# A two-layer diffusion step with 16 experts per layer: TensorE's loop over pairs of experts written out

## Chip, cores and metric

One core of a Trainium2 chip runs the whole step. The metric is the device time of one execution in microseconds; of several executions, their median.

## What is computed

Two layers (`DEPTH = 2`) of a hybrid network on 640 tokens of width 1024: 512 latent tokens and 128 context tokens, all in float32. Each layer has a mixing half (attention, a long convolution, a gated MLP; the change does not touch it) and an expert half. The expert half, cut from the reference:

```python
def _expert_choice(h, router_w, w1, w3, w2):
    ...
    C = max(1, EC_CAPACITY * N // N_EXPERTS)
    aff = jax.nn.softmax((xs @ router_w).astype(jnp.float32), axis=-1)
    gate, idx = lax.top_k(aff.T, C)
    xe = xs[idx]
    he = jax.nn.silu(jnp.einsum('ecd,edf->ecf', xe, w1)) * jnp.einsum('ecd,edf->ecf', xe, w3)
    ye = jnp.einsum('ecf,efd->ecd', he, w2) * gate[..., None].astype(h.dtype)
    out = jnp.zeros_like(xs).at[idx.reshape(-1)].add(ye.reshape(-1, D))
```

There are 16 experts. Each picks its best 64 latent and 16 context tokens (`CAP` = 80 rows), gathers them, and multiplies them with three 1024 x 1024 matrices of its own: w1, w3, w2. So every layer reads 48 matrices of 4 MiB, 201 MB.

## The kernel before

The kernel is written per engine, with semaphores for all order between engines. In the expert half the five instruction streams are these.

**TensorE** (line 1212, `expert`). Line 1177, `products`, is one product of 80 rows with a 1024 x 1024 matrix: 8 chunks of the contraction, each with 12 matmul calls (3 groups of 32 rows by 4 quarters of the columns) at line 1189. In the records each call is two MATMULs and two LDWEIGHTS, so a chunk is 24 MATMULs, a product 192, an expert 576. Four quarters of the array, 32 columns each, work side by side. An expert is: product w3 of this expert, with the 8 transposes of the next expert's gathered rows (line 1208) after its second chunk; product w1 of the next expert; product w2 of this one. Before each half of a product TensorE waits for that half of the weights (line 1182); before w1 it waits for the next rows, scaled (line 1216), and for the silu that empties the banks (line 1217); before w2 for the hidden rows (line 1219). Experts 0 to 13 are seven passes of a hardware loop of two experts each (lines 1225 to 1227); experts 14 and 15 are written out behind it.

**SP** issues the weight loads (lines 580 to 606). Three slots of 4 MiB in SBUF hold w1, w3 and w2; each is filled in two halves of 2 MiB (line 589), and a half is refilled when TensorE has used its last chunk (semaphore `chunk_used`, line 588). SP issues in one fixed order, in a loop over experts: w1 of the expert after, w2 of this one, w3 of the expert after.

**GpSimd** gathers an expert's 80 rows from DRAM (line 665) and adds its results to the residual in DRAM (line 671), in a loop over pairs (line 683); the scatter of an expert must have landed before the next gather is issued (line 674).

**VectorE** (line 2152) scales the gathered rows (lines 2093 to 2101), multiplies the hidden rows and turns them (lines 2123 and 2129) and scales the results (lines 2146 and 2149), in a loop over pairs of experts (line 2159).

**ScalarE** computes the silu (line 1493) and moves a quarter of the results (line 1504), in a loop over pairs that starts with expert 1; expert 0 is written out before it.

The order of the expert half is thus set by TensorE's stream on one side and by the order of the loads on the other; SP's issue depends on TensorE's progress, half by half.

Of the kernel before, what the change touches and what calls it, by code (L numbers as in the profile page):

```python
# [43 lines left out]
EXPERTS = 16  # L44
# [5 lines left out]
PAIRS = EXPERTS // 2  # L50
# [27 lines left out]
def w3_at(e):  # L78

    return e * 3 + 1  # L80


def w1_next_at(e):
    return e * 3 + 2


def w2_at(e):
    return MATS - 1 if isinstance(e, int) and e == EXPERTS - 1 else e * 3 + 3
# [13 lines left out]
def hybrid_prefix_diffusion_step(nc, i, o):  # L102
# [4 lines left out]
    with ExitStack() as ctx:  # L107
# [312 lines left out]
        MOD = [(0, "col"), (1, "col"), (2, "lat"), (2, "ctx"), (3, "col"), (4, "col"), (5, "cap")]  # L420
        ROWS = [(l, j) for l in range(DEPTH) for j in range(ADA)]
        STEPS = [(k, what) for k, (_, j) in enumerate(ROWS) for jj, what in MOD if jj == j]

        def steps_to(k):
# [41 lines left out]
        def width(b):  # L466
            return sum(n for _, n in keys(b)[0])
# [233 lines left out]
        def _(pe):  # L701
# [44 lines left out]
            for l in range(DEPTH):  # L746
# [426 lines left out]
                def products(m, s, e, out, x, between=(None, None)):  # L1173

                    for c in range(KC):

                        if c % HALF == 0:
                            if isinstance(m, int) and m == 0:  # L1180
                                pe.wait_ge(xeT_out, l * (EXPERTS + 1) + c // HALF + 1)
                            pe.wait_ge(half_in[s][c // HALF], (l * EXPERTS + e) * 16 + 16)
                        for g in range(3):
                            for q in range(4):
                                if s == 2:
                                    t, w = (q, g) if q < 3 else (g, q)
                                else:
                                    t, w = g, q
                                mm = pe.matmul(group_out(out, g, slice(q * 32, q * 32 + 32)), x(c, t),  # L1189
                                               slot[s][:, c, w * QUARTER:(w + 1) * QUARTER],  # L1190
                                               start=(c == 0 and g % 2 == 0), stop=(c == KC - 1), skip_group_check=True)
                        mm.then_inc(chunk_used, 1)
                        if c == between[0]:
                            between[1]()

                def rows_of(u):

                    return lambda c, t: xeT[u][:, c, t * 32:t * 32 + 32]
# [5 lines left out]
                def rows_T(u, k):  # L1204

                    pe.wait_ge(xe_in[u], (l * PAIRS + k) * 16 + 16)
                    for c in range(KC):
                        mm = pe.transpose(bank[6 + c // 4][:, (c % 4) * CAP:(c % 4 + 1) * CAP], xe[u][:, c:D:KC],  # L1208
                                          ident[0:CAP, 0:CAP])
                    mm.then_inc(xeT_mm, 1)  # L1210

                def expert(e, u, k, last=False):

                    products(w3_at(e), 1, e, 2, rows_of(u), (None, None) if last else (1, lambda: rows_T(1 - u, k + u)))
                    if not last:
                        pe.wait_ge(xeT_out, l * (EXPERTS + 1) + e + 3)
                        pe.wait_ge(silu, l * EXPERTS + e + 1)
                        products(w1_next_at(e), 0, e + 1, 0, rows_of(1 - u))
                    pe.wait_ge(heT_out, l * EXPERTS + e + 1)
                    products(w2_at(e), 2, e, 4, hidden_of)  # L1220
# [1 line left out]
                pe.wait_ge(top_out, l + 1)  # L1222
                first_rows_T()
                products(0, 0, 0, 0, rows_of(0))
                with pe.Fori(0, PAIRS - 1) as k:
                    for u in range(2):
                        expert(k * 2 + u, u, k)
                expert(EXPERTS - 2, 0, PAIRS - 1)
                expert(EXPERTS - 1, 1, PAIRS - 1, last=True)

                pe.wait_ge(ye_done, l * EXPERTS + EXPERTS)
                for t in range(NT - 1):
# [1080 lines left out]
```

## Time and profile before

| | |
|---|---|
| device time, median of 3 runs | 1998.63 us (1993.74 to 1999.48) |
| the profiled execution's own time | 1992.81 us |
| its span, first to last instruction | 1991.0 us |
| TensorE matmul busy | 1791.2 us, 90% |
| VectorE, ScalarE, GpSimd busy | 34%, 18%, 8% |
| mean granted TensorE clock | 0.946 |
| moved by DMA | 542.55 MB, mean 273 GB/s |
| loads of expert weights | 192 of 2048 KB |
| expert stage of layer 0, of layer 1 | about 418 to 1000 us, 1376 to 1968 us |

The page gives busy time by engine, the chain of work that ended last, and the costliest groups. The chain in order of time gives, for each piece, its start, its length and what it was; "x576" is the number of records in it, and "issue" is time in which the engine waited for nothing that the profile shows. The views by windows give, for a stretch, the busy time of each engine, the granted clock of TensorE as a share of 2.4 GHz, the mean busy share of the 16 DMA engines and what they moved per second.

### The profile page before, as it was taken

To read this page: it belongs to the slowest core of one execution; us is meant where nothing else is said; L and a number is where in the kernel's file an instruction comes from. 1 tells how busy PE (TensorE), PEld (TensorE's weight loads), DVE (VectorE), ACT (ScalarE), POOL (GpSimd) and SP (SyncE) were. 2 spreads that over 40 slices of the span, in tenths; PEclk is the share of its full clock that TensorE was granted. 3 is DMA by queue.
4 is the path that set the end of the run, shared out by engine and by line. 5 is a ranking of instruction groups with operands and counts; after the bars stand their busy time and mean duration, and the time that the engine had idled before them with its cause. 6 is when DMAs were issued, how large, how long until landed. Compare 5 with 4: busy or idle time off the path is not lost.

```text
span 1991.0 us, 50811 instructions
## 1 busy us (share of the span) xinstructions
PE 1791.2 (90%) x23010; PEld 1174.9 (59%) x23010; DVE 672.6 (34%) x1562; ACT 348.6 (18%) x779; POOL 155.3 (8%) x141
## 2 busy tenths in 40 slices
PE   4999988989989989889989998898988988989996
PEld 1776667755545545546557776785644655545563
DVE  4543767531111111111156367664211211211114
ACT  2410364310000000000042125632000000000002
POOL 0100030100000000000002003110000000000000
PEclk9999999989989889889979999998989989989998
DMA  9468201389999889889853722036999889889885
GB/s 343 167 211 314 93 1 43 123 332 408 400 360 386 335 346 386 333 342 385 332 169 124 260 66 85 23 117 254 412 393 387 338 337 386 333 331 390 321 344 192
DMA packets 86724, 542.55 MB, mean 273 GB/s; under 512 B 6928, under 2 KB 12050, under 8 KB 61924
## 3 DMA queue, kind: packets, MB, share of 16 engines
q1 hardware_dynamic: 76036, 502.54, 64.8%
q0 software_dynamic: 10464, 36.51, 6.5%
q8 instruction: 203, 3.33, 0.7%
q14 instruction: 21, 0.17, 0.0%
HBM read 515.50 MB, written 23.53 MB: 271 GB/s over the span
## 4 chain that ended last, share of the span: by engine, by line
PE 83%; DVE 7%; issue 6%; ACT 2%; DMA 1%; POOL 1%; SPq 0%; DVEq 0%; ACTq 0%
PE bank L1189 52%; PE bank L839 10%; PE bank L1026 4%; PE bank L715 2%; PE bank L1208 2%; PE bank L1047 1%; PE bank L985 1%; PE bank L1064 1%; PE bank L742 1%; DMA ring<-in_ada_w 1%; PE bank L970 1%; PE bank L874 1%; PE bank L1097 1%; DVE arena_u L1884 1%; PE bank L733 1%
## 5 line engine op out<-in xcount | busy, mean ns | idle before, releaser
L1189 PE MATMUL bank<-ring,arena_u 128*32 128x256 f32 x12288 | 716.8, 393 | 91.5 <-issue 90.2
L1189 PEld LDWEIGHTS bank<-ring,arena_u 128*32 128x32 f32 x12288 | 403.6, 113 | 385.0 <-issue 134.1
L1189 PE MATMUL bank<-ring,arena_z 128*32 128x256 f32 x6144 | 338.9, 380 | 5.2 <-DVE arena_z L2129 5.2
L1189 PEld LDWEIGHTS bank<-ring,arena_z 128*32 128x32 f32 x6144 | 201.2, 110 | 137.4 <-DVE arena_z L2129 6.1
L2146 DVE SCALAR_TENSOR_TENSOR arena_z<-bank,gateT,gate 80x512 f32<-80x512 f32 (+1 forms) x60 | 34.1, 609 | 546.8 <-PE bank L1189 546.8
L1493 ACT ACTIVATE arena_z<-bank 128x512 f32<-128x512 f32 x30 | 17.9, 597 | 753.4 <-PE bank L1189 753.4
L2123 DVE TENSOR_TENSOR arena_z<-arena_z,bank 128x512 f32<-128x512 f32 x64 | 48.4, 837 | 200.3 <-PE bank L1189 200.3
L671 POOL DMA_INDIRECT x_res<-arena_z,iscat x30 | 43.2, 1439 | 794.8 <-DVE arena_z L2149 794.8
L1026 PE MATMUL bank<-ring_r 128*128 128x512 f32 x320 | 100.8, 396 | 0.3 <-DVE arena_h_r L1873 0.3
L839 PE MATMUL bank<-ring_r,arena_h_r 128*128 128x512 f32 (+1 forms) x240 | 87.1, 363 | 0.0
L1504 ACT ACTIVATE arena_z<-bank 32x256 f32<-32x256 f32 (+1 forms) x90 | 34.0, 378 | 283.2 <-PE bank L1189 282.5
L839 PE MATMUL bank<-ring_r,arena_u_r 128*128 128x512 f32 (+1 forms) x240 | 74.7, 380 | 3.5 <-issue 3.2
L2094 DVE COPY icur<-idxT 80x1 uint32 x28 | 4.2, 150 | 214.3 <-PE bank L1208 214.3
L839 PE MATMUL bank<-ring_r,arena_z_r 128*128 128x512 f32 (+1 forms) x240 | 69.3, 356 | 0.3 <-POOL ring_r L628 0.3
L1026 PEld LDWEIGHTS bank<-ring_r 128*128 128x128 f32 x320 | 58.6, 188 | 12.6 <-DVE arena_h_r L1873 0.8
L1026 PE MATMUL bank<-ring_r,arena_h_r 128*128 128x512 f32 x160 | 62.5, 391 | 0.0
L839 PE MATMUL bank<-arena_h_r,ring_r 128*128 128x384 f32 (+1 forms) x192 | 59.2, 308 | 0.0
L1416 ACT ACTIVATE arena_u<-arena_u,negmax 128x384 f32<-128x384 f32 (+2 forms) x80 | 49.0, 612 | 51.4 <-PE bank L1047 26.0
L839 PEld LDWEIGHTS bank<-ring_r,arena_u_r 128*128 128x128 f32 x240 | 45.7, 200 | 19.5 <-issue 12.8
L715 PE MATMUL bank<-ring,cs 128*32 128x512 f32 x384 | 49.2, 636 | 4.4 <-DMA ring<-in_ada_w 4.3
L839 PEld LDWEIGHTS bank<-ring_r,arena_h_r 128*128 128x128 f32 x240 | 47.1, 196 | 6.5 <-issue 0.2
L1884 DVE CUSTOM_DVE_ANT_0 arena_u<-bank,cst,nsink 128x384 f32<-128x384 f32 (+2 forms) x80 | 47.0, 612 | 9.3 <-PE bank L985 7.9
(305 smaller groups left out, 1913.8 us busy)
## 6 DMA issues: line engine op xcount, KB each, us to landing
ring<-in_exp_w SPq DMA_DIRECT2D x192, 2048.0 KB, 12.8
ring<-in_ada_w SPq DMA_DIRECT2D x24, 2048.0 KB, 10.1
ring<-in_w_in SPq DMA_DIRECT2D x8, 2048.0 KB, 18.8
ring<-in_w_out SPq DMA_DIRECT2D x2, 4096.0 KB, 12.8
x_res<-arena_z POOLq DMA_DIRECT2D x10, 512.0 KB, 3.1
xn_dram<-arena_u POOLq DMA_DIRECT2D x10, 512.0 KB, 2.9
arena_z<-x_res POOLq DMA_DIRECT2D x5, 512.0 KB, 3.6
arena_z<-in_x_sample SPq DMA_DIRECT2D x4, 512.0 KB, 6.2
```

Source lines behind the costliest of these rows:

```text
L671: pool.indirect_dma_start(x_res, bass.IndirectOffsetOnAxis(ap=iscat[u][:, :], axis=0), ye[u] if y is None else y, None, compute_op=ALU.add ...
L715: mm = pe.matmul(out[c % 4 * CT:(c % 4 + 1) * CT, :], cs[:, c, :], slot[s][:, c, h * 512:(h + 1) * 512], start=(c < 4), stop=(c >= 4))
L733: mm = pe.matmul(two[n][0:m, :], sel[:, a:a + m], mrow[k][:, n * 512:(n + 1) * 512], start=True, stop=True)
L839: mm = pe.matmul(pe_out, lhsT, rhs, start=(c == 0 and part == 0), stop=(c == KC - 1 and part == 2))
L1026: mm = pe.matmul(bank[2 - 2 * (n % 2) + x][:, :], m, w, start=(c == 0 and part == 0), stop=(c == KC - 1 and part == 2))
L1189: mm = pe.matmul(group_out(out, g, slice(q * 32, q * 32 + 32)), x(c, t), slot[s][:, c, w * QUARTER:(w + 1) * QUARTER], start=(c == 0 and g ...
L1208: mm = pe.transpose(bank[6 + c // 4][:, (c % 4) * CAP:(c % 4 + 1) * CAP], xe[u][:, c:D:KC], ident[0:CAP, 0:CAP])
L1416: act.activation(prob[n % 2][:, 0:w], sbuf_s[n % 2][:, 0:w], ACT.Exp, bias=negmax[:, b, h:h + 1], scale=-1.0, accum_out=rsum[:, b, h:h + 1 ...
L1504: ins = act.activation(y[g * 32:g * 32 + n, 3 * QUARTER:D], bank[4 + g // 2][96:96 + n, g % 2 * QUARTER:(g % 2 + 1) * QUARTER], ACT.Copy)
L1884: v.tensor_tensor_reduce(out=sbuf_s[n % 2][:, 0:w], in0=bank[4 + n % 2][:, 0:w], in1=mask[:, m0:m0 + w], scale=-SCALE, scalar=nsink[:, h:h ...
L2123: ins = v.tensor_tensor(h.rearrange("p (g c f) -> p g f c", g=2 - n, c=KC), a.rearrange("p (g f c) -> p g f c", g=2 - n, c=KC), bank[2 + n ...
L2146: v.scalar_tensor_tensor(out=y[:, a:b], in0=src, scalar=gate, in1=gate2[:, a:b], op0=ALU.mult, op1=ALU.mult)
```

## The change

TensorE's program for the expert half is written out. The body of the loop, for all 16 experts, is emitted one after the other; the expert's number, its buffer (`e % 2`) and its pair (`e // 2`) are constants. The loads, the other engines' programs and the order of TensorE's own work are the same.

```diff
@@ -1222,11 +1222,8 @@
                 pe.wait_ge(top_out, l + 1)
                 first_rows_T()
                 products(0, 0, 0, 0, rows_of(0))
-                with pe.Fori(0, PAIRS - 1) as k:
-                    for u in range(2):
-                        expert(k * 2 + u, u, k)
-                expert(EXPERTS - 2, 0, PAIRS - 1)
-                expert(EXPERTS - 1, 1, PAIRS - 1, last=True)
+                for e in range(EXPERTS):
+                    expert(e, e % 2, e // 2, last=e == EXPERTS - 1)
 
                 pe.wait_ge(ye_done, l * EXPERTS + EXPERTS)
                 for t in range(NT - 1):
```

`PAIRS` is 8, so the loop made seven passes in each of the two layers.

## Rows read from the trace of the kernel before

**Rows 1.** The page, part 4: the chain that ended last, by line.

```profile
PE bank L1189 52%; PE bank L839 10%; PE bank L1026 4%; PE bank L715 2%; PE bank L1208 2%; PE bank L1047 1%; PE bank L985 1%; PE bank L1064 1%; PE bank L742 1%; DMA ring<-in_ada_w 1%; PE bank L970 1%; PE bank L874 1%; PE bank L1097 1%; DVE arena_u L1884 1%; PE bank L733 1%
```

**Rows 2.** Waits of TensorE: line waited for, us in total, times, longest.

```profile
PE bank L1189 <- issue: 90.2, 24, 5.3
...
PE bank L1189 <- DVE arena_z L2129: 5.2, 2, 2.6
```

**Rows 3.** Chain in order of time, layer 0: start us, us, what.

```profile
433.79 1.04 PE bank L1208 x8
...
466.06 1.05 PE bank L1208 x8
...
644.21 4.84 issue
649.04 3.63 PE bank L1189 x31
652.68 2.29 issue
654.97 2.29 PE bank L1189 x17
657.26 1.20 PE bank L1208 x8
658.46 31.22 PE bank L1189 x576
...
947.33 1.05 PE bank L1208 x8
```

**Rows 4.** The same chain, layer 1.

```profile
1392.35 1.04 PE bank L1208 x8
...
1530.81 5.00 issue
...
1538.59 3.31 issue
...
1913.20 1.05 PE bank L1208 x8
```

**Rows 5.** Windows: stretch, length, PE, PEld, DVE, ACT, POOL, clock, DMA share, GB/s.

```profile
649.04:657.30 8.26, 5.96 (x49) 2.35 (x50) 0.00 (x0) 0.00 (x0) 0.00 (x0) 0.50 0.85 307
```

**Rows 6.** Windows, same columns: stretches with full DMA engines, and a whole pair.

```profile
453.00:485.90 32.90, 32.90 (x604) 19.96 (x600) 5.87 (x11) 2.39 (x6) 2.41 (x2) 1.00 1.01 401
...
520.90:552.00 31.10, 31.10 (x568) 18.79 (x564) 5.87 (x11) 2.01 (x5) 2.34 (x2) 1.00 1.01 413
...
1442.70:1478.60 35.90, 28.16 (x436) 15.35 (x432) 3.96 (x8) 2.01 (x5) 2.35 (x2) 0.81 1.00 387
...
433.79:582.07 148.28, 134.67 (x2338) 79.34 (x2337) 23.52 (x44) 8.02 (x20) 8.55 (x7) 0.95 1.00 402
...
657.26:732.44 75.18, 68.01 (x1170) 39.97 (x1169) 11.75 (x22) 4.01 (x10) 4.70 (x4) 0.93 0.93 355
```

**Rows 7.** SP's waits; line 589 landings, issued 463-475, 1395-1423, 600-645 us.

```profile
SPq L589 <- PE bank L1189: 1015.8, 180, 17.9
...
DMA to landing us min/median/max: 22.2/22.2/22.2
...
DMA to landing us min/median/max: 18.8/19.1/20.5
...
DMA to landing us min/median/max: 11.6/12.9/13.6
```

**Rows 8.** DMA queues, 657.26 to 732.44 us (a pair): packets, MB, share.

```profile
q8 instruction: 11, 0.18, 0.9%
```

**Rows 9.** GpSimd's lines 671 (scatter) and 665 (gather), whole run.

```profile
DMA to landing us min/median/max: 5.1/10.4/11.3
...
DMA to landing us min/median/max: 3.7/10.2/11.7
```

**Rows 10.** Chain in order of time, the last product of layer 0.

```profile
989.95 10.12 PE bank L1189 x181
```

## Prediction

> **What bounds the kernel now.** I read the page first. Its chain of waits puts 52% of the span on the matmuls of line 1189, the expert products [rows 1]. The question is therefore what TensorE waits for there. The list of TensorE's waits answers it: 90.2 us in 24 pauses of at most 5.3 us are put down to "issue" (the engine waited for no semaphore or transfer that the profile knows), and the largest other wait of the line is 5.2 us in 2 pauses for VectorE's hidden rows [rows 2]. No weight load is in that list. The expert stage is bound by TensorE's own stream, and the stream has holes.
>
> The chain in order of time shows where the holes are. An expert without one takes 32.27 us from transposes to transposes (466.06 - 433.79) [rows 3]. A pause comes after every second expert: at 644.21 the engine stops 4.84 us, runs 31 matmuls in 3.63 us, stops 2.29 us, runs 17 in 2.29 us, and only after the transposes is it back at its pace. In layer 1 it is 5.00 and 3.31 us [rows 4]. There are six such places per layer, 12 in all, two pauses each, which makes the 24. They stand where the pair loop jumps back: seven iterations give six jumps. The borders between experts inside an iteration, and the two of each layer that fall through (into experts 14 and 15), have none.
>
> The second part of the loss is the clock. Between 649.04 and 657.30 the granted clock was 0.50, the lower of its two levels (1.2 and 2.4 GHz), after an idle time of 4.84 us [rows 5]. The 48 matmuls of the two broken chunks take 5.92 us there; at the rate of a whole expert (31.22 us / 576 = 54.2 ns each [rows 3]) they would take 2.60 us.
>
> **The change, part by part.**
>
> *The jumps.* Twelve go. By steps, for the turn at 644.21: 4.84 + 2.29 us of pause, 5.92 - 2.60 = 3.32 us of slow matmuls, 1.20 - 1.05 = 0.15 us of slow transposes [rows 3], together 10.6 us. By layers, which takes in that turns differ: in layer 0 the stretch from expert 0's transposes to expert 14's is 947.33 - 433.79 = 513.54 us, and 14 experts of 32.27 us are 451.78 us, so the turns cost 61.8 us [rows 3]. In layer 1 it is 1913.20 - 1392.35 = 520.85 us, so 69.1 us [rows 4]. **Sum removed: 130.8 us.** Of this, 90.2 is pause [rows 2] and 40.6 the slow clock behind it.
>
> *Instructions.* The same matmuls, loads, transposes and semaphore waits run in the same order; waits against a register become waits on constants, and register and branch instructions go. No engine waited for these inside an expert, so I book nothing. The code is longer, but the instruction stream already is: a pair of experts in the middle of the loop reads 11 instruction packets [rows 8], so the body is read again on every pass. The straight code reads the same amount in order.
>
> *The other loops' turns.* The loops of ScalarE, SP, GpSimd and VectorE stay. ScalarE's turns fall one expert later than TensorE's (its first expert is written out), where TensorE runs through: they cost nothing already. VectorE's and GpSimd's turns lie under TensorE's pauses, a cover that goes. VectorE must have the next rows scaled before the w1 product: that starts six chunks after the transposes, 6 x 1.30 = 7.8 us (31.22 / 24 chunks). A turn as dear as TensorE's 4.84 us leaves 3 us for its three instructions, so 0 us on the path, with little to spare. GpSimd's scatter and gather land 11.3 and 11.7 us after issue at most [rows 9]; one after the other, 23 us from the end of an expert, are due 32.27 + 2.6 us after it. Also 0 us.
>
> *The weight loads.* This is the cover that matters. SP refills each half slot when its last chunk is used and nearly always waits for TensorE (1015.8 us in 180 waits [rows 7]), so loads follow TensorE's pace. A half slot is used again five halves later, 5/6 x 32.27 = 26.9 us. At the start of each layer the loads are late: the half issued at 463.7 landed 22.2 us later, in layer 1 the slowest of the first ones 20.5 us. That leaves 26.9 - 22.2 = 4.7 and 6.4 us. Later, after some turns, it is 11.6 to 13.6 us [rows 7]: the turns let the loads catch up.
>
> What do they need without turns? A pair now moves 355 GB/s x 75.18 us = 26.69 MB, 13.34 MB per expert [rows 6]. In 32.27 us that is 413 GB/s. What can they get? Where the DMA engines were full: 401 (453.0 to 485.9 us), 413 (520.9 to 552.0), 387 (1442.7 to 1478.6), and over the longest stretch, 148 us, 402 GB/s [rows 6]. I take 400, by the longest: 33.35 us per expert, 1.08 us more than TensorE needs. Over experts 2 to 14 this makes 13 x 1.08 = 14.0 us of lag, less about 5.5 us of slack at the start: 8.5 us per layer. **Given back: 17 us.** The ends: at 413 GB/s nothing; at 387, 34.47 us per expert, 13 x 2.20 - 5.5 = 23 us per layer, 46 us. The waits would be about a microsecond per expert, in pieces. Whether they lower the clock is bounded by one row: after a wait of 2.6 us before the last product of layer 0, 181 matmul records took 10.12 us, 55.9 ns each, so nothing to speak of [rows 10]. Even if it fell, TensorE would run late while the loads catch up, and the loads' pace would still set the end.
>
> *A rule against it.* The trace shows full DMA engines moving 402 GB/s over 148 us [rows 6]. The Trainium skill, page "DMA: Bandwidth & Descriptors", section Specifications, gives an HBM limit of about 358 GB/s per core (half of a stack) beside a fabric ceiling of 435. By 358 an expert would need 13.34 / 358 = 37.3 us and the change would win some 9 us. The trace speaks against 358 for this kernel, which runs alone.
>
> **The sum.** 1992.81 us (the profiled execution's own time; span 1991.0) - 130.8 + 17 = 1879 us. That execution was 5.8 us under the median of the runs shown (1998.63), and below their lowest; I add 5 us for this and forecast 1884 us. What sits outside the expert stage is not touched.
>
> **The rivals.**
> 1. *The loads stay hidden.* They reach 413 GB/s on the whole, as in one stretch [rows 6]; 1992.8 - 130.8 = 1862, with the 5 us up to 1867. For it: no product waited for a load in the first 62 us of a layer, when they ran late. Against: the mean over the longest stretch is 402. Chance 0.20.
> 2. *The loads are already the bound,* or nearly: with the queue never empty the rate falls below 387, as far as the mean of a pair now, 355 GB/s. Then an expert takes 37.6 us and a pair 75.2 us as before; only the fall-through experts are unaltered and the gain is a few us: about 1984 by the rule above, 1950 at 370 GB/s. For it: the pair's 355 lies near that limit. Against: the DMA engines were only 0.93 busy in that pair. Chance 0.09.
> 3. *The pause isn't the jump's.* Something else happens every second expert. By the Trainium skill, page "Advanced Engine Details and Errata", section Control Flow Timing, a compare-and-branch takes about 108 ns: by that alone twelve would be 1.3 us. Rows show 4.84 us and then a second pause a chunk later, which fits code that has to be fetched after a jump, and none where the loop isn't re-entered. If the pauses stayed: 1991 us, no change. Chance 0.05.
> 4. *Slower: the instruction stream falls behind in straight code.* Its packets share the 16 DMA engines with weight loads whose queue would now never drain; each new block would be waited for. At about five packets per expert [rows 8] it reads 160 in two layers; from 131 / 160 = 0.82 us per block on the change loses. At the 2.29 us of the second pause [rows 3] it would be 1992.8 - 131 + 366 = 2228 us. Against: from 453.0 to 485.9 us the DMA engines were 1.01 busy with a 22 us queue [rows 6, 7], and the chain of that stretch has no pause. Chance 0.04.
>
> **How the numbers follow.** The forecast, loads that bind late in each layer, has 0.62: from a few us given back to 46, 1862 to 1908, and up to 1913 with the 5 us. With rival 1 this is 0.82, so the range is 1861 to 1915. Faster by over 0.3% (6 us, about what a measurement of this kernel can tell) are the forecast and rivals 1 and 2: 0.91. Rival 3 is within 0.3%: 0.05. Rival 4 is slower: 0.04.
>
> **What would show it.** The 24 "issue" waits of line 1189 gone, and each layer's chain one row of transposes every 32.27 us for the first four or five experts; then a new wait, line 1189 on the weight load, 10 to 50 us in total, and experts of about 33.4 us. DMA share near 1.0 through both stages, median landing of the expert loads up from some 13 to well over 20 us, granted clock at 1.00 there and the mean up from 0.946. Expert stretches (transposes 0 to 14) of about 460 us. It would be wrong if pauses of several us stay under "issue" (rivals 3, 4), if no load is ever waited for (1), or if experts take over 35 us (2).

## The result and the profile after

| | before | after |
|---|---|---|
| median of the runs | 1996.18 us (4 runs, 1990.35 to 1999.48) | 1892.59 us (4 runs, 1888.76 to 1894.58) |
| ratio after / before | | 0.9482, 95% interval 0.9452 to 0.9511 |
| the profiled execution | 1992.81 us | 1893.56 us |
| mean granted clock | 0.946 | 0.975 |
| TensorE matmul busy | 1791.2 us | 1758.0 us |
| landing of an expert's weight half, median | 12.8 us | 26.6 us |

The change makes the kernel 103.6 us faster in the medians, 99.2 us in the profiled executions. The forecast was 1884, the range 1861 to 1915.

TensorE's waits after the change (line waited for, us in total, times, longest). The group of 90.2 us under "issue" [rows 2] is gone, and a wait for weight loads that did not exist before leads the list; VectorE's hidden rows are as they were:

```profile
PE bank L1189 <- DMA ring<-in_exp_w: 24.0, 25, 2.0
...
PE bank L1189 <- DVE arena_z L2126: 5.2, 2, 2.6
```

The chain in order of time, layer 0 (start us, us, what). It is the same view as [rows 3]:

```profile
430.45 1.04 PE bank L1208 x8
...
462.71 1.04 PE bank L1208 x8
...
494.97 1.05 PE bank L1208 x8
...
527.24 1.05 PE bank L1208 x8
528.28 23.49 PE bank L1189 x432
...
551.94 27.39 DMA ring<-in_exp_w
...
579.46 5.42 PE bank L1189 x96
...
627.10 1.04 PE bank L1208 x8
...
896.93 1.04 PE bank L1208 x8
```

For four experts the transposes come every 32.26 us: 430.45, 462.71, 494.97, 527.24. Then the chain leaves TensorE. It goes back through a weight load of 27.39 us to SP, which issued it at 551.9, when TensorE had freed the half slot. From here on TensorE is stopped for a short time in nearly every w2 product. Expert 6's transposes begin at 627.10 and expert 14's at 896.93: 269.83 / 8 = 33.73 us per expert. In layer 1 it is 1543.61 and 1813.88, 33.78 us.

The windows over experts 0 to 14 of each layer (stretch, length, busy time of PE, PEld, DVE, ACT, POOL, clock, DMA share, GB/s):

```profile
430.45:896.93 466.48, 454.78 (x8177) 282.82 (x8177) 82.21 (x154) 28.05 (x70) 30.70 (x27) 1.00 1.01 401
...
1344.98:1813.88 468.90, 455.94 (x8177) 281.81 (x8177) 82.30 (x154) 28.05 (x70) 31.55 (x27) 1.00 1.01 400
```

The two stretches were 513.54 and 520.85 us [rows 3, 4] and are 466.48 and 468.90: 99.0 us of the 99.2. The DMA engines are full from end to end, and the granted clock is at its upper level throughout, although TensorE now stops some 12 times per layer.

The landing times of the weight loads issued from 600 to 860 us, where they had been 11.6 to 13.6 us for a similar stretch [rows 7]:

```profile
DMA to landing us min/median/max: 26.0/26.9/28.2
```

A half slot is used again 26.9 us later at TensorE's own pace, and 28.1 us later at 33.73 us per expert, so there is no slack left.

The page's count of instruction packets (each 16 KB of program), before and after:

```profile
q8 instruction: 203, 3.33, 0.7%
```

```profile
q8 instruction: 181, 2.97, 0.6%
```

These are 22 fewer for 12 jumps fewer.

### The profile page after: what moved, and what is told of

Same layout as the page of the kernel before. It is cut to its first block, busy times and chain, and to the rows that moved or that the text cites. A ratio compares the mean times of both kernels' runs of the same rounds, so it can differ in the third digit from the quotient of the medians.

```text
span 1891.7 us, 50683 instructions
## 1 busy us (share of the span) xinstructions
PE 1758.0 (93%) x23010; PEld 1182.2 (62%) x23010; DVE 672.7 (36%) x1562; ACT 348.4 (18%) x779; POOL 155.3 (8%) x141
## 4 chain that ended last, share of the span: by engine, by line
PE 62%; DMA 26%; DVE 7%; issue 2%; ACT 2%; POOL 1%; SPq 0%; DVEq 0%; ACTq 0%
PE bank L1189 30%; DMA ring<-in_exp_w 25%; PE bank L839 11%; PE bank L1026 5%; PE bank L715 2%; PE bank L1047 1%; PE bank L985 1%; PE bank L1064 1%; PE bank L742 1%; PE bank L1097 1%; PE bank L970 1%; PE bank L1208 1%; PE bank L874 1%; DVE arena_u L1881 1%; PE bank L733 1%
## 5 line engine op out<-in xcount | busy, mean ns | idle before, releaser
L1189 PE MATMUL bank<-ring,arena_u 128*32 128x256 f32 x12288 | 679.7, 381 | 3.0 <-DMA ring<-in_exp_w 1.6
L1189 PEld LDWEIGHTS bank<-ring,arena_u 128*32 128x32 f32 x12288 | 398.6, 110 | 266.3 <-DMA ring<-in_exp_w 5.9
L1189 PE MATMUL bank<-ring,arena_z 128*32 128x256 f32 x6144 | 341.7, 381 | 28.1 <-DMA ring<-in_exp_w 22.4
L1189 PEld LDWEIGHTS bank<-ring,arena_z 128*32 128x32 f32 x6144 | 213.5, 110 | 154.2 <-issue 27.7
L665 POOL DMA_INDIRECT arena_z<-xn_dram,icur x30 | 27.5, 916 | 284.6 <-issue 270.4
## 6 DMA issues: line engine op xcount, KB each, us to landing
ring<-in_exp_w SPq DMA_DIRECT2D x192, 2048.0 KB, 26.6
```

The source lines that it names most:

```text
L665: pool.indirect_dma_start(xe[u], None, xn_dram, bass.IndirectOffsetOnAxis(ap=icur[u][:, :], axis=0))\
```

## The experiments

**The same jumps, to near code.** Are the pauses the price of a jump, or of a jump to code that is no longer at hand?

```diff
                 for e in range(EXPERTS):
+                    if e % 2 == 0 and 2 <= e <= 12:
+                        with pe.Fori(0, 2):
+                            pe.wait_ge(const_in, 32)
                     expert(e, e % 2, e // 2, last=e == EXPERTS - 1)
```

> Straight code as after the change, but at the six places per layer where the loop used to turn there is an empty loop of two passes around one wait that is already met: the same number of jumps back (12), to code a few instructions away. Theory (what costs is that the code at the target must be read in again, not the jump): as after, 1892 us within 3 us, no pause over 1 us. Rival (the jump itself, or the emptying of the engine's queue at a branch, costs the 7 us): pauses of about 5 us at the 12 places come back and the time is about 1990 us.

Measured: 1890.03 us, 0.9482 of the kernel before (0.9462 to 0.9502), the ratio of the changed kernel. The loops ran (50743 instructions in the trace against 50683), and the view of TensorE's waits has no "issue" at line 1189 at all:

```profile
PE bank L1189 <- DMA ring<-in_exp_w: 20.4, 26, 1.9
```

Twelve jumps back to the near target cost nothing that shows, and no instruction packet more than the straight code (181). What cost 7 us was that the target's code was a pair of experts away and had to be read in again. Two things show that the pauses are this reading. One is the number of packets: 203 with twelve far jumps, 190 with the four of the next experiment, 181 with none or with near ones. The other is when they arrive, read from the start and end of each single packet in the traces. At the turn at 644.21 [rows 3] one packet runs from 646.35 to 647.37 and TensorE goes on at 649.04; the next ends at 653.52, in the second pause, and TensorE goes on at 654.97. It is so every time: all 24 pauses of the kernel before, the 6 of the kernel with passes of four and the 24 of the loop kernel with light loads end 1.2 to 1.7 us after an instruction packet has ended. This also speaks against the rival that near jumps leave open, that computing the waits' values in registers at each turn is what costs.

**Fewer turns.** The loop comes back with passes of four experts.

```diff
-                for e in range(EXPERTS):
-                    expert(e, e % 2, e // 2, last=e == EXPERTS - 1)
+                with pe.Fori(0, 3) as k:
+                    for u in range(4):
+                        expert(k * 4 + u, u % 2, k * 2 + u // 2)
+                for e in range(12, EXPERTS):
+                    expert(e, e % 2, e // 2, last=e == EXPERTS - 1)
```

> TensorE's loop comes back with passes of four experts (three passes, experts 12 to 15 written out): 2 jumps back per layer instead of none (after) or 6 (before). Theory (a turn costs a fixed 10.9 us: two pauses and the slow clock behind them; the weight loads then catch up during it, so what the loads give back vanishes): 1993 - 131 + 4 x 10.9 = about 1905 us, with 8 issue pauses and next to no wait for weight loads. Rival (turns and load waits add up, because the load waits come from something a turn does not relieve): 1893 + 44 = about 1937 us, with 20 us or more of waits for loads left.

Measured: 1898.48 us, 0.9528 (0.9502 to 0.9553); the runs lie from 1890.52 to 1905.25. The rival (1937) is out. The chain around a turn in layer 0 and one in layer 1:

```profile
424.77 1.05 PE bank L1208 x8
...
551.24 5.58 issue
...
560.37 1.68 issue
...
899.05 1.05 PE bank L1208 x8
...
1472.03 5.09 issue
1477.12 5.06 PE bank L1189 x48
```

There is not one wait for weight loads in its list. In layer 0 expert 0's transposes are at 424.77 and expert 14's at 899.05, 474.3 us, which is the 451.8 us without a stop and 22.5 us for the two turns. With four experts between turns the loads take nothing back: the stretch is as long as the turns make it. In layer 1 it is 466.8 us (1345.57 to 1812.35), 15.0 us for two turns, 2.1 us less than the straight kernel's. So a turn and the load waits do not add up. A turn takes over the wait that the loads would have caused. The two stretches together are 5.7 us longer than the fully straight kernel's, as the medians are by 5.9. In layer 1 the turns have one pause instead of two (six pauses in all, not eight), so the four turns cost 37.5 us and not 43.6, and the time came in below 1905.

**The loads made lighter**, in both kernels. Every w1 load of a layer after the first brings half of its columns.

```diff
+                        m = D if s or before is None else D // 2
-                        sp.dma_start(slot[s][:, h * HALF:(h + 1) * HALF, :],
+                        sp.dma_start(slot[s][:, h * HALF:(h + 1) * HALF, 0:m],
...
```

> Straight code; every w1 load after a layer's first brings only half of its columns (the rest of the slot keeps older weights, so part of the product is of other data). This takes a sixth of the expert weight bytes away and nothing else. Theory (in the straight kernel the DMA engines' rate sets the pace from expert 4 on): the waits for weight loads vanish, experts take 32.27 us throughout, 1893.6 - 31.8 = about 1862 us. Rival (waits come from the fixed time that a load needs or from the order of issue, not from the rate): w2 is still waited for, 1880 us or more.

> The kernel before with the same lighter w1 loads (a sixth of the expert weight bytes left out). Theory (before the change the loads were wholly hidden, the turns alone bound the stage): the same time as before within 3 us. Rival (the loads already cost time before, through slower instruction reads at the turns): pauses get shorter and the time falls by 5 us or more.

Measured: straight 1860.73 us, 0.934 (0.9314 to 0.9366), no wait for a weight load, transposes every 32.27 us through all experts. The loop kernel 1993.54 us, 0.9992 (0.9978 to 1.0005), its pauses 87.6 us in 24:

```profile
PE bank L1190 <- issue: 87.6, 24, 4.7
```

Together these separate the two terms of the forecast. With light loads, taking the turns out is worth 1993.5 - 1860.7 = 132.8 us (forecast 130.8). With the real ones it is worth 103.6. The loads cost the loop kernel nothing and the straight one the rest.

**GpSimd's transfers made small.** Twice: gathers and scatters both, and the scatter alone. Both leave the results of the experts out of the residual; the first also leaves the experts with stale rows.

```diff
                 def gather(u):
-                    pool.indirect_dma_start(xe[u], None, xn_dram,
-                                            bass.IndirectOffsetOnAxis(ap=icur[u][:, :], axis=0))\
-                        .then_inc(xe_in[u], 16)
+                    pool.dma_start(xe[u][:, 0:128], xn_dram[0:CAP, 0:128]).then_inc(xe_in[u], 16)
...
-                    pool.indirect_dma_start(x_res, bass.IndirectOffsetOnAxis(ap=iscat[u][:, :], axis=0),
-                                            ye[u] if y is None else y, None, compute_op=ALU.add).then_inc(scattered, 16)
+                    pool.dma_start(x_res[0:CAP, 0:128], (ye[u] if y is None else y)[:, 0:128]).then_inc(scattered, 16)
```

> Straight code; the gathers from expert 1 on and all scatters move 80 rows of 128 numbers instead of 1024, by plain transfers (so experts compute on stale rows and their results are not added; the times of the products are unchanged). It takes 0.57 of 13.3 MB per expert away, 4%, and all indirect transfers. Theory (GpSimd's transfers are what puts the rate from 425 GB/s, seen before the first of them, to 394): the loads are hidden, no waits, about 1862 us. Rival (the weight loads alone already run at 394 GB/s when the queue is full): 12.7 MB / 394 = 32.3 us, waits of a few us left, 1862 to 1868. If the waits stay above 15 us, neither holds.

> Straight code; all scatters write 80 rows of 128 numbers by a plain transfer instead of adding 80 rows of 1024 by an indirect one (the experts' results are not added to the residual); gathers as they are. Theory (GpSimd's two transfers of an expert cost the loads alike, by their bytes): half of the lag of 1.6 us per expert goes, 13 x 0.8 - 5 = 5 us per layer are left, about 1872 us, waits of 5 to 10 us. Rival (the adding scatter costs nearly all of it): no waits, 1861 us. Rival (the gather costs nearly all): 1885 us or more.

Measured: both small 1860.65 us, 0.9331 (0.9304 to 0.9359); the scatter alone 1857.59 us, 0.9305 (0.9285 to 0.9325). Neither has a wait for a weight load, and experts take 32.27 us. The first run did not tell its two theories apart (1862 against 1862 to 1868). The second did: the scatter alone is enough. The DMA queues from 624.3 to 894.3 us, eight experts (packets, MB, share of the 16 engines' time), in the changed kernel:

```profile
q1 hardware_dynamic: 7007, 102.09, 92.3%
q0 software_dynamic: 1536, 5.24, 7.9%
```

and with the small scatter:

```profile
q1 hardware_dynamic: 7263, 105.73, 96.0%
q0 software_dynamic: 1024, 2.95, 3.4%
```

The full scatter brings 2.3 MB more to the queue of GpSimd in this stretch, 2.1% of all bytes, but takes 4.5% of the DMA engines' time: 270 us x 0.045 / 8 = 1.5 us per expert. (With the small scatter the stretch holds 8.4 experts. Taken per expert, the queue needs 2.7 us and 1.1 us.) The lag of the loads was 33.73 - 32.27 = 1.46 us. It does not go wholly. With the small scatter the last parts of the loads still come every 32.5 us (33.8 with the full one, see below), 0.2 to 0.3 us more than TensorE takes, and the slack at the start covers that for the 13 experts. Of the 1.5 us, the adding, the indirect addresses and the bytes (40 KB instead of 320) were not tried apart.

**The first load earlier.** If what is given back is lag minus the slack at the start, more slack should win. In the changed kernel SP holds a layer's first w3 load until gathers 0 and 1 have landed. Four variants move it. Behind gather 0 alone (run twice):

```diff
                         if s == 1 and before is None and not h:
-                            for u in range(2):
-                                sp.wait_ge(xe_in[u], l * (PAIRS * 16) + 16)
+                            sp.wait_ge(xe_in[0], l * (PAIRS * 16) + 16)
```

> Straight code; SP issues the first w3 load of a layer once gather 0 has landed, not gather 1 too: 3.2 us earlier. Theory (the give-back per layer is lag minus slack at the start): 3 us less per layer, 1892.6 - 6 = about 1886 us. Rival (the slack at the start doesn't matter, waits are spread by some other cause, or the loads slow gather 1 and this costs as much): 1892 us as after the change.

> The changed kernel itself, unaltered, so that the earlier first w3 load can be compared with it on one chip: 1890 to 1893 us, 20 to 25 us of waits for weight loads.

> The first w3 load of a layer behind gather 0 alone, again, beside the changed kernel itself. Theory: 5 to 6 us below it, as the waits fell by 6.0 us in the first run of it. Rival: within 2 us, the waits that went are paid elsewhere.

Measured: first 1889.60 us, 0.946 (0.9439 to 0.9482), waits for loads 18.0 us. Then, on one chip, the changed kernel 1893.37 us, 0.9459 (0.9439 to 0.9479), and this one 1880.12 us, 0.942 (0.9393 to 0.9448), waits 20.0 and 19.5 us. It is the fastest version run that computes the same. But the two intervals touch. From transposes 0 to transposes 14 it takes 463.8 and 464.0, then 462.8 and 465.5 us, against 466.5 and 468.9, then 465.3 and 464.9 for the changed kernel. That is 2.4 us per layer on the mean, but only 1.0 in the pair on one chip, and the changed kernel differs from itself by up to 4 us. So a gain here is possible and not shown. Nor do the 13 us of the last comparison show one: of the 13.6 us between the profiled executions, 7.7 lie behind expert 14's transposes of layer 1. There the last sums ran as in the changed kernel's first execution, 5.43 us, and not as in straight_again, 16.76 us (last section).

Further ahead: one half before the rows' way to DRAM, both halves before it, and both right behind it (that is, before gather 0).

```diff
                 fill(0, "exp_w1", 0, None)
+                fill(1, "exp_w3", 0, None, (0,))
...
-                fill(1, "exp_w3", 0, None)
+                fill(1, "exp_w3", 0, None, (1,))
```

(for the first of them, with the second half behind gather 0; in the others `fill` of both halves stands at the place named, without the wait for gathers)

> Straight code; the first half of w3 of expert 0 is loaded right behind w1, in the time before the gathers in which the DMA engines are half idle, and its second half after gather 0. Theory: 8 us more slack per layer at the start, so 14 to 16 us less in all: about 1877 us, waits for loads under 10 us. Rival (the load delays the normalised rows' way to DRAM and gather 0, which stand on the chain into the stage): up to 4 us per layer of it is paid back, 1885 us.

> Straight code; both halves of w3 of expert 0 are loaded right behind w1, before the normalised rows are out. Theory: 11 us more slack per layer, waits for loads nearly gone, but gather 0 now runs beside the second half and lands in 8 to 10 us instead of 3.7: 1892.6 - 22 + 2 x 5 = about 1880 us. Rival (gather 0 is not slowed, or the chain has room for it): 1870 us. Rival on the other side (the rows' way to DRAM is held up by a full queue): 1890 us or more.

> Straight code; the first w3 loads of a layer are issued when the normalised rows are in DRAM, 2 us before gather 0 instead of after gathers 0 and 1: 9 us earlier, and out of the rows' way. Theory (lag minus slack, and gather 0 beside a load takes 8 to 10 us instead of 3.7): waits for loads under 10 us, chain into the stage 5 us longer per layer, in all 1892 - 16 + 10 = about 1886 us. Rival (gather 0 gets its share of the DMA engines quickly and is hardly slower): 1877 us. Rival on the other side (gather 0 waits behind the whole queue, 10 us or more): 1893 us or more.

Measured: 1893.65 us, 0.950 (0.9478 to 0.9522); 1896.40 us, 0.9481 (0.9456 to 0.9507); 1894.46 us, 0.9482 (0.9466 to 0.9498). None beats the changed kernel. The waits were 17.0, 19.5 and 16.3 us, against 24.0 and 20.0 in the two executions of the changed kernel, so they fell by less than forecast or not at all, and the way into the stage grew: transposes 0 of layer 0 came at 431.6, 434.4 and 434.1 us, against 430.5 and 430.0. With the first half early, GpSimd holds gather 0 for the rows' way to DRAM, where in the changed kernel it was waiting for VectorE's list:

```profile
POOL arena_z L679 <- DMA xn_dram<-arena_u: 13.0, 1, 13.0
```

and TensorE's wait at line 1148, for the lists, which was 6.0 us in 2, is

```profile
PE bank L1148 <- DVE pair L2076: 14.4, 2, 7.6
```

With both halves right behind the rows, the wait for the lists is unchanged and TensorE waits for gather 0 instead, 7.0 us in 2. That is the rival on the other side. A transfer ahead of its time pays for its place in the queue, and here the chain into the stage pays it.

## Why the prediction was right, and where it was off

**The turns.** Their removal was put at 130.8 us: 61.8 in layer 0, 69.1 in layer 1. The light pair of runs gives 132.8, and 451.7 us per stretch of 14 experts as computed. The order of the argument held: pauses from the list of waits, their place from the chain, and the 40 us of slow clock behind them, which no list of waits shows, from the length of whole stretches.

**The other loops' turns** were booked at nothing, and are nothing: in the straight kernels with hidden loads every expert takes 32.27 us, while VectorE, ScalarE, GpSimd and SP still loop.

**The loads** were the step that was off in size. The mechanism came as written: no wait for the first four experts, then a wait for the weight load, 24.0 us in 25 pieces of 2.0 us at most, loads that land after 26.9 us, full DMA engines, a clock of 1.00. But 17 us were to be given back, and the two stretches gave 466.48 - 451.78 = 14.7 and 468.90 - 451.78 = 17.1, together 31.8. The mis-sized term is the lag less the slack at the start, and both parts were off.

The first part is the pace. The prediction divided the bytes of an expert by the mean rate of all 16 DMA engines: 13.34 MB / 400 GB/s = 33.35 us. As a mean this was right: the view gives 401 and 400 GB/s. But TensorE waits for the whole of a load. Each load raises its semaphore 16 times, by one part of it at a time. In straight_again, where the trace has every one of these records, all 19 stops of over 0.35 us for a load end 0.04 to 0.14 us after the last of the 16 parts. The parts do not keep step. Of the first half of expert 2's w1 (changed kernel, layer 0) they landed within 1.7 us, at 462.9 to 464.6 us; of the same half of expert 14, eight landed at 857.6 to 859.1 and eight at 869.2 to 870.5. From expert 4 to 14 the early eight came every 32.9 us, the late eight every 33.8, the mean of the 16 every 33.3. TensorE's pace, 33.73 and 33.78 us, is that of the late half, so the lag was 1.46 and 1.51 us and not 1.08. This is also why the view counts more than 48 loads in eight experts (102.09 MB, and 48 x 2.10 = 100.7): the early parts had run ahead into later loads. The same split is there in layer 1, in straight_again, in near_jump and with the small scatter. Why eight parts are faster is not shown. The lag is a difference of two near numbers: 1.1% of the pace is a third of the 1.08 us.

The second part is the slack at the start. It was read as 4.7 and 6.4 us from loads that landed after 22.2 and 20.5 us; those issued at the same places (layer 0, at 460.3 us; layer 1, at 1374.8) now landed after 23.5 and 24.2 us, which leaves 3.4 and 2.7. This is not a property of the change: in straight_again, the same kernel, they landed after 20.7 and 18.8 us, and its two stretches are 465.3 and 464.9 us. With both parts, 13 x 1.46 - 3.4 = 15.6 and 13 x 1.51 - 2.7 = 16.9, together 32.5 us against 31.8. The pace in this sum is read from the same stretches, so it shows how the terms add up and is no second test.

The sum with the measured term is 1992.8 - 130.8 + 31.8 = 1893.8, and the profiled execution is 1893.56. The prediction's own sum was 1879, before it added 5 us for the distance of that execution from its median. The execution of the changed kernel was no faster than its median, so these 5 us had no counterpart there, and that they brought the forecast nearer, to 1884, is luck.

**The rivals.** That loads stay hidden (1) is out by 24.0 us of waits, that they were the bound already (2) by the loop kernel with light loads, 0.9992. The "some 9 us" and the 1984 us for 358 GB/s don't come out of the forecast's own steps, which give 13 x 5.0 - 5.5 = 59 us per layer, a gain of 12 us and 1981; nothing else rests on it. The 358 GB/s of the Trainium skill ("DMA: Bandwidth & Descriptors", Specifications) did not apply to this kernel, which moved 400 GB/s for 466 us. That the pause is not the jump's (3) turned out half true: it is not the branch, which by the Trainium skill ("Advanced Engine Details and Errata", Control Flow Timing) is about 0.1 us and in near_jump costs nothing that shows. It is the far target. The Trainium skill says this too ("Runtime: NRT & Kernel Launch", Instruction fetch mechanics): a taken branch to a target outside the window held forces a fetch before execution goes on. The runs agree with it: every pause ends 1.2 to 1.7 us after a packet of instructions. The prediction took the straight code to read as much as the loop; it reads 22 packets less. That straight code would be read too slowly (4) is out: no "issue" pause with full DMA engines for 466 us.

## What to carry to other kernels

TensorE's loop over two experts, some 2,300 matmuls and weight loads long, paid 10.9 us on the mean at every turn: 7.5 us of pause for reading its start again, and 3.4 us for the lower clock after it. A loop of one instruction paid nothing. Such a price is in the gaps at the turn, found by lining the pauses up with the loop. Before booking such a gap as a gain, work out what else ran on during it: here the weight loads caught up in every turn, and without turns they were the next bound. Where that bound lies within a few per cent of the engine's own pace, the loss is a difference of two near numbers, and one per cent in either moves it by a third. And a mean rate over all DMA engines is not the pace at which whole loads land: here the one gave 33.3 us per expert and the other 33.8.

## What had not been expected of the hardware

The 16 parts of a weight load drift apart while the DMA engines are full: 1.7 us between the first and the last at expert 2, 12.8 us at expert 14. In the kernel before, whose loads catch up at every turn, it was 3.7 us at expert 14.

An indirect scatter that adds, 80 rows of 4 KB, costs the 16 DMA engines 1.5 us more of their time than a plain one of 80 rows of 512 bytes, about twice what the bytes between them would take at the mean rate (2.29 MB / 8 / 400 GB/s = 0.7 us).

A turn can have one pause instead of two: in layer 1 of the kernel with passes of four, 5.09 us and then 48 matmuls in one piece. In layer 0 of the same kernel, two. The loops do the same work and lie at different places in the program; whether that is the cause is not shown.

Two executions of one kernel differed by 6 us behind the last product. In the changed kernel the last sums (line 742) of the execution profiled first ran at the upper level, with a clock of 1.00 from 1870.31 to 1875.74; in straight_again, with a clock of 0.52 from 1865.99 to 1882.75. The way from the end of layer 1's products to the end of the span is 23.2 us in the one and 29.1 us in the other (1868.5 to 1891.7, 1864.2 to 1893.3). A difference of a few us between two variants can be this, and needs the stage's own length beside the total.
